# A two-block model on one core: the order of work around the state-space scan

## The reference

```python
zxbcdt = x @ in_proj                      # z 2048, xs 2048, B 1024, C 1024, dt 32
xbc = silu(causal_depthwise_conv(xbc, conv_w, conv_b))
dt = softplus(dt + dt_bias); A = -exp(A_log)
# per chunk of 128 tokens and head (32 heads of 64, 8 groups of 4 heads):
cum = cumsum(dt * A); decay = exp(cum[t] - cum[s]) where s <= t
y = ((C @ B.T) * decay * dt) @ xs + (terms of the state before)
y = (y + D * xs) * silu(z)
yg = y.reshape(b, s, 8, 256)
yg = yg * rsqrt(mean(yg * yg) + 1e-5)     # a norm per group
out = (yg * norm_g) @ out_proj
h = layer_norm(alpha * h + out)
```

## Time and profile before

| | |
|---|---|
| median of 3 runs | 1315.45 us (1314.27 to 1315.6) |
| the profiled execution | 1315.27 us |
| its span in the profile | 1313.5 us |
| TensorE busy | 1265.9 us, 96% |
| VectorE busy | 928.2 us, 71% |
| ScalarE busy | 679.5 us, 52% |
| GpSimd busy | 83.7 us, 6% |
| HBM read | 225.68 MB, 173 GB/s over the span |

### The profile page before, as it was taken

How to read it: one execution, slowest core, us unless ns; L and a number is a source line. 1 busy time by engine, 2 the same in 40 slices (tenths; PEclk the granted TensorE clock), 3 DMA queues, 4 the chain that set the end, 5 groups by cost and what they waited for, 6 DMA issues and landing times. The chain is left out here.

```text
span 1313.5 us, 18633 instructions
## 1 busy us (share of the span) xinstructions
PE 1265.9 (96%) x7688; PEld 1119.9 (85%) x7688; DVE 928.2 (71%) x1288; ACT 679.5 (52%) x851; POOL 83.7 (6%) x94
## 2 busy tenths in 40 slices
PE   7999999999999999999999989999999899999997
PEld 7878999989977888889997877888888877888886
DVE  5566757775447556677967876788878747788877
ACT  5654444444444444446766564466654464565652
POOL 2000000100000000000003340100000100000000
PEclk9999999999999999999999998999999999999999
DMA  8654555756435666546555544655554532655551
GB/s 278 209 177 134 183 156 166 238 166 206 161 98 161 192 191 192 193 132 193 162 180 195 186 150 139 197 191 189 192 193 138 183 125 92 201 192 189 188 187 47
DMA packets 159748, 227.98 MB, mean 174 GB/s; under 512 B 5517, under 2 KB 122001, under 8 KB 159536
## 3 DMA queue, kind: packets, MB, share of 16 engines
q1 hardware_dynamic: 156544, 216.68, 51.3%
q0 software_dynamic: 2816, 9.52, 2.2%
q10 hardware_dynamic: 304, 0.59, 0.1%
HBM read 225.68 MB, written 1.10 MB: 173 GB/s over the span
## 5 line engine op out<-in xcount | busy, mean ns | idle before, releaser
L1232 DVE TENSOR_TENSOR wlo<-raw,whi 128x2048 fp32r<-128x2048 f32 (+3 forms) x188 | 419.7, 2244 | 118.8 <-ACT whi L789 118.2
L789 ACT ACTIVATE whi<-raw 128x2048 fp32r<-128x2048 f32 (+3 forms) x203 | 378.1, 1876 | 21.2 <-DMA raw<-in_w_xkv 6.6
L2012 PE MATMUL psum<-h_both,whi 128*128 128x512 f32 x714 | 254.7, 396 | 0.0
L1980 PE MATMUL psum<-h_both,whi 128*128 128x256 f32 x704 | 201.2, 286 | 0.0
L2011 PE MATMUL psum<-h_both,wlo 128*128 128x256 f32 x714 | 199.6, 280 | 0.3 <-DVE h_both L1274 0.3
L1982 PE MATMUL psum<-h_both,wlo 128*128 128x256 f32 x704 | 199.7, 284 | 0.0
L1981 PE MATMUL psum<-h_both,whi 128*128 128x256 f32 x704 | 199.7, 284 | 0.0
L1980 PE MATMUL psum<-whi,r_hi 128*128 128x512 f32 (+1 forms) x464 | 182.6, 393 | 6.2 <-DVE r_lo L1274 3.2
L1982 PE MATMUL psum<-whi,r_lo 128*128 128x512 f32 (+1 forms) x464 | 179.1, 386 | 0.0
L1981 PE MATMUL psum<-wlo,r_hi 128*128 128x512 f32 (+1 forms) x464 | 179.1, 386 | 0.0
L2012 PEld LDWEIGHTS psum<-h_both,whi 128*128 128x128 f32 x714 | 134.1, 188 | 27.5
(11 more groups left out here) (325 smaller groups left out, 1835.2 us busy)
## 6 DMA issues: line engine op xcount, KB each, us to landing
raw<-in_ffn_up SPq DMA_DIRECT2D x44, 1024.0 KB, 5.1
raw<-in_w_in SPq DMA_DIRECT2D x32, 1024.0 KB, 5.7
raw<-in_ssd_in_proj SPq DMA_DIRECT2D x24, 1024.0 KB, 5.4
raw<-in_ffn_down SPq DMA_DIRECT2D x22, 1024.0 KB, 4.9
raw<-in_w_up SPq DMA_DIRECT2D x16, 1024.0 KB, 5.5
raw<-in_w_down SPq DMA_DIRECT2D x16, 1024.0 KB, 5.0
raw<-in_w_xkv SPq DMA_DIRECT2D x8, 1024.0 KB, 5.5
raw<-in_ssd_out_proj SPq DMA_DIRECT2D x8, 1024.0 KB, 5.0
```

The lines of the kernel that those rows point to most:

```text
L789: A(whi[u % SLOTS][:, 0:kt * n], raw[u % SLOTS][:, 0:kt * n], ACT.Copy).then_inc(hi_split, 1)
L1232: V.tensor_tensor(wlo[s][:, 0:kt * n], raw[s][:, 0:kt * n], whi[s][:, 0:kt * n].bitcast(F32), ALU.subtract).then_inc(lo_split, 1)
L1980: M(o, a_hi, b_hi, start=start, stop=False)
L2012: return M(b[:, :], w_hi_k, h_both[:, :, k, :], start=False, stop=k == kt - 1)
```

## The change

Five edits, all in the scan and the units ahead of it. The input transposes of unit j are run between the two halves of unit j + 2 instead of behind unit j + 1; the seventh stays behind the last unit. The ring's places are put in another order: the own tile, the two in `rows`, the three in the arena; heads 0, 1 and 2 are loaded in the first call and 3, 4 and 5 in the second. Gate and statistics stand in front of the head's product. The last group set is gated in two halves, the first in the step of the last head. The last two pairs of output transposes move up by one step. GpSimd's load of `ln_mix_b_2` into `rows` waits for the last head's product and stands behind the last set's power.

```diff
-    steps += [("none", 0)] * (SSD_PER_UNIT * (SSD_UNITS - 2) - 2 - len(steps)) + [("yT", 6), ("yT", 7)]
+    steps += [("none", 0)] * (SSD_PER_UNIT * (SSD_UNITS - 2) - 3 - len(steps)) + [("yT", 6), ("yT", 7), ("none", 0)]
...
-        dec = [dec0[:, :]] + [room(14336 + TRI * b, TRI) for b in range(3)]
-        dec[2:2] = [rows[:, 1, TRI * b:TRI * b + TRI] for b in range(2)]
+        dec = [dec0[:, :]] + [rows[:, 1, TRI * b:TRI * b + TRI] for b in range(2)] + [room(14336 + TRI * b, TRI) for b in range(3)]
...
-                elif h == 1:
+                elif h == 3:
                     wait_bank(sp, ("xsN", 7))
...
-            rows_at = {at[("zz", 0, 0)] + SLOTS - 1: [0, 2, 3], at[("zz", 0, 1)] + SLOTS: [1, 4, 5]}
+            rows_at = {at[("zz", 0, 0)] + SLOTS - 1: [0, 1, 2], at[("zz", 0, 1)] + SLOTS: [3, 4, 5]}
...
-            pool.wait_ge(ssd_y, SSD_HEADS - 4)
-            row(1, w["ln_mix_b_2"][0])
             rsqrt(4)
             group_power.append(powers[0])
+            pool.wait_ge(ssd_y, SSD_HEADS)
+            row(1, w["ln_mix_b_2"][0])
...
+            def gate_half(q, g):
+                wait_drained(dve, ("y", 2 * q + g))
+                for t in range(NT):
+                    wait_drained(dve, ("zz", q, t))
+                y = yN[q % 2][:, :, 256 * g:256 * g + 256]
+                mark(V.tensor_tensor(y, y, szN[:, :, MIX * q + 256 * g:MIX * q + 256 * g + 256], ALU.mult))
...
                     if what == "head":
-                        dve.wait_ge(s_exp, h + 1)
-                        b = wait_bank(dve, ("CB", h // 4))
-                        V.tensor_tensor(dec[h % SSD_RING], dec[h % SSD_RING], b[:, 0:TRI], ALU.mult)\
-                            .then_inc(done(("CB", h // 4)) if h % 4 == 3 else s_w, 1)
                         if h > 8 and h % 8 == 2:
                             add_sums(2 * q - 1)
                             gate(q - 1)
                         if h > 8 and h % 8 == 3:
                             group_stats(q - 1)
+                        dve.wait_ge(s_exp, h + 1)
+                        b = wait_bank(dve, ("CB", h // 4))
+                        V.tensor_tensor(dec[h % SSD_RING], dec[h % SSD_RING], b[:, 0:TRI], ALU.mult)\
+                            .then_inc(done(("CB", h // 4)) if h % 4 == 3 else s_w, 1)
...
+                        if h == SSD_HEADS - 1:
+                            gate_half(3, 0)
                     if what == "tail":
                         add_sums(7)
-                        gate(3)
+                        gate_half(3, 1)
                         group_stats(3)
...
             for j in range(8):
-                b_unit(at[("xc", j)], h_hi, h_lo, one(("xc", j)))
-                if j >= 1:
-                    xs_transpose(j - 1)
+                b_unit(at[("xc", j)], h_hi, h_lo, one(("xc", j)),
+                       between=(lambda c: xs_transpose(j - 2) if c == 1 else None) if j >= 2 else None)
+            xs_transpose(6)
```

## The result

The changed kernel takes 1304.99 us (median of four executions, 1303.48 to 1305.17) where the kernel before takes 1314.86: a ratio of 0.9923, 95% interval 0.9908 to 0.9939, so 9.9 us faster. The profiled execution has a span of 1303.2, 10.3 less than before. The forecast was 1306.4 in a range of 1303.3 to 1309.8: the sign and the range held. A gain of 9.0 was forecast where 9.9 was measured; the other 0.6 of the distance between 1306.4 and 1304.99 is the base, since the forecast started from 1315.45. The terms inside did not all come out; two large errors happened to stand against each other.

The account below looks back on a forecast made before the run. TensorE, working 96% of the span, was taken as the bound, so only its waits and low clock could yield time. Gains 4.2 + 3.4 + 1.1 + 0.3 = 9.0 off 1315.45 gave 1306.4 us, range 1303.3 to 1309.8.

Parts of the forecast that it names:

- Input transposes: First input transposes of the scan: moved half a unit on, 2.7 of wait and 1.5 of clock go, gain 4.2 us.
- Ring order: Head 1's product in the scan: its row comes earlier, 1.7 of wait and 1.7 of low clock go, gain 3.4 us.
- Gating and statistics: VectorE's chain before the gated output's transposes: one product leaves each of three sets, gain 1.1 us, between 0 and 1.4.
- The three waits: TensorE's waits at the transposes of the gated output (L2537), 4.9 us together before, expected at some 1.1 to 1.5 each.
- Tail: Last gating to the layer norm: 2.0 of 4.6 comes through, 1.7 lost to clock; gain 0.3 us, between 0 and 2.0.
- a wait of 2.9: New TensorE wait at the layer norm behind the last unit, as VectorE still owes splits; low clock expected after it.
- The mid-norm wait of 1.38: VectorE's wait for TensorE in the middle of the layer norm, counted as gone: 1.38 of the 2.0 us coming through.
- The low clock: TensorE at 1.2 instead of 2.4 GHz behind long waits: 1.5 us regained at inputs, 1.7 at ring, 1.7 lost at norm.
- a case for one place: Second rival: the clock stays up through the new wait at the layer norm, 1.7 us more gained, 1304.7 us, chance 0.25.

## Why the prediction was right or wrong

**Input transposes: right.** 4.2 forecast, 4.15 measured. TensorE comes to the new place just as the SiLU is done (648.79 + 0.63 = 649.42; the transposes start at 649.48), and the later sets wait for nothing.

**Ring order: right against the profile of before, wrong as a price of the edit.** 3.4 forecast and 3.34 read. Head 1's wait fell from 1.91 to 0.16 and head 3 was covered. But the 1.7 of low clock in the term are not the price of the wait: with the inputs alone moved, 1.63 was waited with the clock at 1.00, and 1.65 with the ring undone. The edit itself is worth 1.5.

**Gating and statistics: the term that was mis-sized.** The forecast took "0.47 for each of three sets", less a mask beside the gates, 1.1; it is 3.7. The mask was there (the first set's gates took 1.83 instead of 1.57), and 0.47 left each chain; what the runs show for this, 0.9 to 1.0, is close to the 1.1. What was missed is the power on GpSimd, 0.9 a set, 2.7 in all: I costed the moved product only in the chain that it left and did not ask what now runs beside GpSimd instead of it. The three waits were expected at 1.1 to 1.5 and came at 0.3 to 0.4. The trace of before had all that was needed: four powers of 1.93 to 1.96, each begun a little behind a split with two SBUF operands. The Trainium skill (SBUF — State Buffer, section "Who interferes with whom") says that a VectorE instruction with two SBUF inputs contends with a GpSimd one that reads SBUF, and calls the ports that they share an exclusive lock. The prediction applied this to the gates and the masks, not to the power. The traces agree for the power that comes second (1.93 to 1.96 against 1.02 to 1.04). For a VectorE instruction that comes second they are divided: the split that begins 0.31 behind a running power takes 1.22, as it does elsewhere, while the one that begins 0.05 behind a mask takes 1.77.

**Tail: right in mechanism, sized by chance.** The forecast said that of 4.6 at the last unit only 2.0 can come through, as VectorE reaches the norm late behind its splits, and that a wait of 2.9 turns up there, with 1.7 lost to the clock, 0.3 net. The wait is 2.59, the low clock costs 1.5, and 0.68 is left in the first profile; moving one split shows the cause, as the wait falls to 0.40. The 2.0 was too much. The old tail takes 47.6 in the kernel before, with low clock from 808 to 816, and 46.1 with the clock up; the new one takes 45.5 with the clock up. So 1.5 of the 2.1 is clock in the kernel before and 0.6 is the edit, and that 0.68 is left with the clock down again is chance. The mid-norm wait of 1.38, which the forecast counted as gone by the edit, belongs to that low clock: with the old tail it is 0.16 where the low clock ends at 804, and there is none where the clock is up.

**The low clock: a step that failed in kind.** The forecast took low clock as following from long waits ("after 2.71 and 3.17 the clock fell, so I take it that it falls here too"). It followed 2.59 in one execution of the changed kernel and not 2.60 in another; not 3.15 with the inputs alone; not 1.04 in the attention before, but 1.05 after. That last one is the 1.6 us which the sum did not have. No run here shows what decides it; they do show that the length of the wait alone does not. The Trainium skill (TensorE: Matmul & The Clock Gate, Part 1) says that the window of the monitor that gates the clock runs free of the kernel's start; the two profiles of the changed kernel fit that. The prediction gave this 0.25 as a case for one place; it holds for every place at once. So 9.0 came near 9.9 (10.3 between the two profiles) because 2.6 too little at the gating and 1.6 not foreseen in the attention stood against each other; 0.4 too little at the tail is most of the rest. That nearness was luck.

What stays open: where the low clock falls in each of the executions that were timed without a profile, and so how a difference of medians under 2 us splits into work and clock.

## What to carry to other kernels

When an instruction is moved, price both neighbourhoods: what runs ahead of it, and what now stands beside the short instruction of another engine that a chain hangs on. Here a GpSimd power of 1.0 us took 1.93 to 1.96 whenever VectorE had begun a two-operand SBUF split 0.16 before it, and putting a PSUM reader or an idle slot there was worth 0.9 at each of four places. Compare kernels by where the same instruction stands in two traces, counted from an instruction ahead of the change, before comparing medians, and book low clock behind a wait as a chance, not as a cost of that wait.

## What the runs showed of the hardware that was not expected

- A power of 128x4 on GpSimd takes 1.02 to 1.04 when VectorE stands or runs a PSUM reader as it begins, and 1.93 to 1.96 when a 1.22 us split of VectorE began 0.16 before it; the split takes 1.22 in both orders. A split that began 0.05 behind a mask of GpSimd (128x256) took 1.77.
- With the same waits to 0.01 us, TensorE's clock fell behind a wait of 2.6 in one execution and not in the other; it cost 1.5. Executions of one kernel stood in two groups, 1303.5 to 1304.3 and 1305.0 to 1305.5 us, with mean clocks of 0.997 and 0.995.
- A wait of about 1.05 at a product of narrow operands was followed by low clock in seven of fourteen profiles, each time with some 1.7 us lost by it (as in 6 us at a mean clock of 0.72), and by none in the others.
